# Gate sums and first maxima inside the convolution units, and r, k, v as three products of rounded parts

## The reference

```
# layer 0: gated short convolution beside forgetting attention (8 heads x 64)
z = x @ w_in;  ax, a_b, a_c, q, k, v, fl = split(z)
y_a  = a_b * conv3(a_c * ax)                        # causal, width 3
logf = log_sigmoid(fl + b_f);  cum = cumsum(logf)
s = q.k / 8 + cum[query] - cum[key], masked;  o = softmax(s) @ v
y = concat(y_a, o) @ w_out
# layer 1: RWKV-7 time mixing (16 heads x 64)
xr, xw, xk, xv, xa, xg = (x + (x_prev - x) * mu[n] for n in range(6))
r = xr @ w_r;  k = xk @ w_k;  v = xv @ w_v          # 1024 x 1024 each
# w, a, g: products through a narrow hidden layer; then a recurrence over the positions
# every layer ends in a SwiGLU channel mixer and a gated embedding
```

## Time and profile before

| what | value |
|---|---|
| median of 3 runs | 4127.3 us (4125.62 to 4127.95) |
| profiled execution | 4123.89 us |
| its span | 4122.3 us |
| TensorE busy | 3726.8 us, 90% |
| VectorE busy | 1461.3 us, 35% |
| ScalarE busy | 831.4 us, 20% |
| POOL busy | 203.2 us, 5% |

### The profile page before, as it was taken

One profiled execution on the slowest core, in us unless ns is written; L12 is line 12 of the kernel. 1 busy time (PEld: TensorE's weight loads), 2 busy tenths in 40 slices (PEclk: granted clock), 3 DMA queues, 4 the chain that ended last, 5 costly groups with the idle time before them and its releaser, 6 DMA issues.

```text
span 4122.3 us, 64833 instructions
## 1 busy us (share of the span) xinstructions
PE 3726.8 (90%) x27922; PEld 3201.6 (78%) x27922; DVE 1461.3 (35%) x1951; ACT 831.4 (20%) x1107; POOL 203.2 (5%) x345
## 2 busy tenths in 40 slices
PE   7998899899999998878998868889797999999977
PEld 4996337789999998754564537878496999999967
DVE  3123544342212223432211645555635222222352
ACT  2000232210000001223311423333322000000021
POOL 0001000000000000000000211111100000000000
PEclk9998999999999999986999989999999999999989
DMA  2212002111121131002222652211311112112211
GB/s 87 73 53 85 21 21 76 70 45 41 46 83 48 46 124 47 29 21 107 96 74 103 258 187 54 53 45 52 139 42 69 46 36 73 62 46 87 77 37 69
DMA packets 75064, 291.43 MB, mean 71 GB/s; under 512 B 9368, under 2 KB 11688, under 8 KB 71128
## 3 DMA queue, kind: packets, MB, share of 16 engines
q0 software_dynamic: 36528, 165.56, 11.1%
q1 hardware_dynamic: 38336, 122.87, 9.6%
HBM read 211.77 MB, written 76.62 MB: 70 GB/s over the span
## 4 chain that ended last, share of the span: by engine, by line
PE 72%; DVE 8%; ACT 2%; issue 2%; DMA 1%; POOL 0%; DVEq 0%; ACTq 0%; POOLq 0%
PE ps L443 47%; PE ps L417 11%; DVE A L1436 2%; PE ps L836 2%; PE ps L845 2%; DVE B L1436 1%; PE ps L750 1%; PE ps L457 1%; DVE H L1517 1%; PE ps L796 1%; DVE A_r L1493 1%; PE ps L475 1%; DVE B L1900 1%; PE ps L859 1%; PE ps L823 1%
## 5 line engine op out<-in xcount | busy, mean ns | idle before, releaser
L443 PE MATMUL ps<-A_r,TM_r 128*128 128x364 f32 x2736 | 605.3, 329 | 0.0
L443 PE MATMUL ps<-H_r,W_r 128*128 128x364 f32 (+1 forms) x2616 | 576.3, 328 | 0.0
L443 PE MATMUL ps<-H_r,TM_r 128*128 128x364 f32 x2352 | 520.8, 329 | 19.0 <-DVE A_r L1493 19.0
L417 PE MATMUL ps<-B,W 128*128 128x364 f32 (+1 forms) x1488 | 469.7, 477 | 24.9 <-DVE B L1436 24.9
L443 PEld LDWEIGHTS ps<-A_r,TM_r 128*128 128x128 f32 x2736 | 476.0, 189 | 0.0
L443 PEld LDWEIGHTS ps<-H_r,W_r 128*128 128x128 f32 (+1 forms) x2616 | 453.5, 187 | 1.8
L417 PEld LDWEIGHTS ps<-B,W 128*128 128x128 f32 (+1 forms) x1488 | 282.5, 190 | 207.6 <-issue 28.7
L443 PEld LDWEIGHTS ps<-H_r,TM_r 128*128 128x128 f32 x2352 | 408.0, 188 | 23.7 <-issue 14.5
L443 PE MATMUL ps<-B_r,DW_r 128*128 128x364 f32 x2112 | 408.8, 329 | 0.0
L443 PE MATMUL ps<-B_r,W_r 128*128 128x364 f32 x1824 | 404.6, 330 | 0.0
L443 PEld LDWEIGHTS ps<-B_r,DW_r 128*128 128x128 f32 x2112 | 358.8, 188 | 0.0
(11 more groups left out here) (279 smaller groups left out, 4146.4 us busy)
## 6 DMA issues: line engine op xcount, KB each, us to landing
W<-in_wgu SPq DMA_DIRECT2D x88, 512.0 KB, 3.6
W<-in_wdown SPq DMA_DIRECT2D x32, 384.0 KB, 3.1
W<-in_wrkv SPq DMA_DIRECT2D x24, 512.0 KB, 3.7
W<-in_wdown SPq DMA_DIRECT2D x32, 320.0 KB, 2.9
d_h<-H POOLq DMA_DIRECT2D x16, 546.0 KB, 3.0
d_y<-TM POOLq DMA_DIRECT2D x16, 546.0 KB, 3.6
A<-d_y POOLq DMA_DIRECT2D x16, 546.0 KB, 7.8
H<-d_h POOLq DMA_DIRECT2D x2, 4368.0 KB, 22.7
```

What stands on the lines that cost most here:

```text
L417: ins = nc.tensor.matmul(ps[0:cols, NCH * s + c, 0:CH], W[0:rows, slot, j * cols:(j + 1) * cols], xs[n][0:rows, c * CH:(c + 1) * CH], star ...
L443: ins = nc.tensor.matmul(ps[0:cols, NCH * s + c, 0:CH], w[:, j * cols:(j + 1) * cols], x[k1][:, c * CH:(c + 1) * CH], start=(k1 == 0 and n ...
```

## The change

**Layer 0.** The gate's log f and running sums move ahead of the convolution loop on ScalarE and VectorE, and `turn_sums` stands between the third and the fourth convolution unit. The filler products go. Behind each of the last nine convolution units TensorE computes one piece of the first pair's scores, in banks 6 and 7, and VectorE reduces it among the steps of the convolution; pieces 9 to 11 stay behind the last unit, and both `spread` calls follow them. POOL sends the sums and loads the bias rows of the first pair between the convolution's stores; the other pairs' rows stay behind the last unit. The gate's buffers move from A and TM to B and DW.

**Layer 1.** r, k and v use `split_unit`. The upper parts of the mixed activations are written to H, the remainders in place in B. H is therefore stored to memory when layer 0 ends and loaded again when the recurrence has begun. VectorE splits every weight tile; in the v loop the split stands behind the first instruction of a pair. Results of r and k leave through two buffers where there were four, and so do those of v.

The diff, cut to its core:

```diff
-                 "down": (DWr[:, 0, :], DWr[:, 1, :])}
+                 "down": (DWr[:, 0, :], DWr[:, 1, :]),
+                 "rkv": (TMr[:, 2, 0:KT * P], TMr[:, 3, 0:KT * P]),
+                 "value": (Br[:, 20, 0:KT * P], Br[:, 21, 0:KT * P])}
...
-        BIAS = [Af[:, SEQ * h:SEQ * h + SEQ] for h in range(HF)]
-        TOP = [[Af[:, HF * SEQ + 16 * b + 8 * h:HF * SEQ + 16 * b + 8 * h + 8] for h in range(2)] for b in range(2)]
+        BIAS = [Bf[:, 12 * T + SEQ * h:12 * T + SEQ * h + SEQ] if h < 2 else Af[:, SEQ * h:SEQ * h + SEQ] for h in range(HF)]
+        full, cump = Bf[0:HF, 12 * T:12 * T + NALL], Bf[0:HF, 12 * T + NALL:12 * T + NALL + SEQ]
+        DWf = DW[:, :, :].rearrange("p a n -> p (a n)")
...
-        CKT = Tf[:, 3200:3200 + 8 * (8 + NBLK)].rearrange("p (k h) -> p k h", h=HF)
-        zcol = Tf[:, 3500:3501]
+        CKT = Bf[:, o_ + 32:o_ + 32 + 8 * (8 + NBLK)].rearrange("p (k h) -> p k h", h=HF)
+        zcol = Bf[:, o_ + 240:o_ + 241]
...
             split_unit(xh, xl, cols=HF)
-            for j in range(3 * NA):
-                split_unit(xh, xl)
...
                 qb, n0, n = ROWS[j]
+                bank = 0 if p else 6
                 if pieces(p, j):
                     pe.wait_ge(S["s_read"], pieces(p, j))
-                if halves(p, int(j >= FIRST_HALF[0])):
+                else:
+                    pe.wait_ge(S["ckt_ready"], 1)
+                if p:
                     pe.wait_ge(S["mb_read"], halves(p, int(j >= FIRST_HALF[0])))
...
+            for j in range(3 * NA):
+                split_unit(xh, xl)
+                if j == 2:
+                    turn_sums()
+                if j >= 3:
+                    scores(0, j - 3)
+
             pe.wait_ge(S["read0"], t.val("read0"))
             pe.wait_ge(S["read1"], t.val("read1"))
-            full_clock(16)
-            turn_sums()
-            for j in range(len(ROWS)):
+            for j in range(3 * NA - 3, len(ROWS)):
                 scores(0, j)
-                if j == FIRST_HALF[0] - 1:
-                    spread(0, 0)
+            spread(0, 0)
             spread(0, 1)
             turned(0, 0)
             turned(0, 1)
...
+            xh = [Hr[:, j, :] for j in range(KT)]
+            xlow = [[Br[:, 8 * b + j, :] for j in range(KT)] for b in range(2)]
+            enter(t, "rkv")
             for n in range(2):
-                pe.wait_ge(S["xn_ready"], t.up("xn_ready", KT))
-                xs = X[(n + 1) % 2]
-                dense8(KT)
...
+                t.up("xn_ready", KT)
+                split_units(KT, xh, xlow[(n + 1) % 2])
...
+            enter(t, "value")
+            pe.wait_ge(S["xl_ready"], t.up("xl_ready", KT))
...
-                    unit([KT], xs)
+                    split_unit(xh, xlow[1])
...
+            z, e = B[0:HF, 15, :], DWf[0:HF, 0:T]
+            s, mm, rd = t.unit()
...
             for c in range(NA):
+                if c == 1:
+                    turned_sums()
...
-            turned_sums()
...
+            def upper_mixed(b, kt):
+
+                act.wait_ge(S["xn_ready"], t.val("xn_tmp", kt + 1 - KT))
+                nc.scalar.activation(Hr[:, kt, :], B[:, 8 * b + kt, :], ACT.Copy).then_inc(S["xh_ready"], 1)
...
             mix(0)
-            stage()
+            act.wait_ge(S["hs_out"], 16)
+            for n in range(KT):
+                staged(n, 4)
+                upper_mixed(1, n)
             mix(2)
-            stage()
-            mix(3)
-            stage()
+            for n in range(KT):
+                staged(n, 2)
+            for n in range(KT):
+                upper_mixed(0, n)
+            for n in range(KT):
+                if n < 2:
+                    mix(3, 4 * n, 4 * n + 4)
+                staged(n, 2)
+            for n in range(KT):
+                upper_mixed(1, n)
...
+            lf, e = B[0:HF, 15, :], DWf[0:HF, 0:T]
+            step(nc.vector.memset(zcol, 0.0))
+            dve.wait_ge(S["lf_e"], 1)
+            step(stt(lf, lf, 0.0, e, ALU.min, ALU.subtract))
+            dve.wait_ge(S["cum_in"], t.up("cum_in", 16))
+            step(nc.vector.tensor_copy(full[:, PAST:NALL], lf[:, S0:T]))
+            nc.vector.tensor_tensor_scan(cump, lf[:, P0:P0 + SEQ], zcol[0:HF].to_broadcast([HF, SEQ]), 0.0, ALU.add,
+                                         ALU.subtract)
+            step(nc.vector.tensor_tensor_scan(full, full, zcol[0:HF].to_broadcast([HF, NALL]), 0.0, ALU.add, ALU.subtract))
+            step(nc.vector.tensor_scalar(cump, cump, -8.0, None, ALU.mult))
+            nc.vector.tensor_scalar(full, full, -8.0, None, ALU.mult).then_inc(S["cum_ready"], 1)
...
             for c in range(NA):
                 s, mm, rd = t.unit()
                 dve.wait_ge(S[f"read{s}"], rd)
                 split_chunk()
+                if c:
+                    reduced(0, 3 * c - 3)
...
                 step(nc.vector.memset(TM[:, 2, 0:PAD], 0.0))
+                if c:
+                    reduced(0, 3 * c - 2)
...
                 if c < NA - 1:
                     split_chunk()
...
+                if c:
+                    reduced(0, 3 * c - 1)
...
             dve.wait_ge(S["ckt_ready"], 1)
-            for j in range(len(ROWS)):
+            for j in range(3 * NA - 3, len(ROWS)):
                 reduced(0, j)
-            nc.vector.memset(zcol, 0.0)
+            dve.wait_ge(S["s_read"], len(ROWS))
+            dve.wait_ge(S["logf_out"], 1)
+            dve.wait_ge(S["conv_out"], 32 * NA)
+            nc.vector.memset(B[:, 12:16, 0:PAD], 0.0)
+            nc.vector.memset(B[:, 12:16, S0 - PAD:S0], 0.0)
...
+            def lower_mixed(b):
+
+                for kt in range(KT):
+                    dve.wait_ge(S["xh_ready"], t.up("xh_ready"))
+                    nc.vector.tensor_tensor(Br[:, 8 * b + kt, :], B[:, 8 * b + kt, :], Hr[:, kt, :],
+                                            ALU.subtract).then_inc(S["xl_ready"], 1)
+                    t.up("xl_ready")
...
+            def split_weights(done):
+
+                slot, landed = t.chunk()
+                if done:
+                    dve.wait_ge(S["mm_done"], done)
+                dve.wait_ge(S[f"w{slot}"], landed)
+                w, wh = W[:, slot, 0:KT * P], wh_of(t)
+                step(nc.vector.tensor_copy(wh, w))
+                nc.vector.tensor_tensor(Wr[:, slot, 0:KT * P], w, wh, ALU.subtract).then_inc(S["wl_ready"], 1)
...
+            enter(t, "rkv")
+            mix(0, 1)
+            mix(1, 4)
+            mix(2, 5)
+            mix(3, 0)
+            split_weights(0)
+            lower_mixed(1)
+            split_weights(0)
+            mix(4, 2)
+            for m in range(2, KT + 1):
+                split_weights(mm0 + 27 + m - 1)
+            lower_mixed(0)
+            split_weights(mm0 + 27 + KT)
+            dve.wait_ge(S["mm_done"], read_by[3])
+            step(nc.vector.memset(B[:, 8:16, 0:1], 0.0))
+            mix(5, 3, 0, 4)
+            split_weights(mm0 + 27 + KT + 1)
+            mix(5, 3, 4, 8)
+            for m in range(KT + 3, 2 * KT):
+                split_weights(mm0 + 27 + m - 1)
+            enter(t, "value")
+            dve.wait_ge(S["xs2"], 96)
+            dve.wait_ge(S["xs3"], 96)
+            lower_mixed(1)
...
                     step(nc.vector.tensor_scalar(tmpA, L["a"], vec[:, V["ka"], bass.ds(pair, 1)],
                                                  kab[:, bass.ds(pair, 1)], ALU.mult, ALU.add))
+                    split_weights(0)
                     dve.wait_ge(S["key_scaled"], t.up("key_scaled"))
...
+            dve.wait_ge(S["hs_in"], 16)
             channel_mixer(1)
...
+            pool.dma_start(full[:, 0:PAST], I["clogf"]).then_inc(S["cum_in"], 16)
...
+            pool.wait_ge(S["cum_ready"], 1)
+            pool.dma_start(d_cum, cump).then_inc(S["cum_out"], 16)
+            pool.dma_start(d_cums, full).then_inc(S["cum_out"], 16)
+            store(O["logf"], B[0:HF, 15, :])
+            pool.wait_ge(S["cum_out"], 32)
+            pool.wait_ge(S["ckt_done"], 1)
+            bias(0)
+            pool.wait_ge(S["out_done"], t.val("out_done"))
+            pool.sem_inc(S["logf_out"], 1)
             for c in range(NA):
...
             pool.wait_ge(S["mm_done"], t.val("mm_done"))
-            pool.dma_start(Af[0:HF, 5000:5000 + PAST], I["clogf"]).then_inc(S["cum_in"], 16)
...
+            for i in range(1, NA):
+                pool.wait_ge(S["bias_in0"], 32 * i)
+                bias(i)
...
+            pool.wait_ge(S["h_ready"], 24)
+            pool.dma_start(d_h, H[:, :, :]).then_inc(S["hs_out"], 16)
             pool.wait_ge(S["shift_in"], 1)
...
             for name in "rk":
-                keep(name)
+                with t.loop(4, mm_done=2, read0=1, read1=1, xs0=16, xs1=16) as i:
...
             double_chunk(2)
+            pool.wait_ge(S["hs_out"], 16)
+            pool.dma_start(H[:, :, :], d_h).then_inc(S["hs_in"], 16)
             with t.loop(3, u_done=8, tok_done=8, zi0=96, zi1=96) as i:
```

(53 more changed lines are left out.)

119 lines of the change are left out of this document (42 added, 77 removed).

## The result

The changed kernel takes 4086.44 us (median of 3 runs, 4082.80 to 4092.95) where the kernel before takes 4127.3: a ratio of 0.990 (0.9885 to 0.9912). The prediction was 4026, with a range of 4010 to 4052. The sign was right; 60 us of the gain are missing. The profiled execution took 4082.8.

A forecast was written before the change was run, and what follows sets the result against it. TensorE, 72% of the span, bounds it: stages pay only where it computes or stands on the chain. 41.3 + 38.1 + 21.8 = 101.2 off 4123.9 gives 4022.7; with the median 3.4 higher, 4026, range 4010 to 4052.

The forecast's parts named there:

- H's reload: Recurrence: loading H again takes 22.7 us, fits between two of POOL's chunk loads and costs nothing.
- A: v loop: transfers set its period, so it gives nothing; 4048, chance 0.14.
- B: First stage: half the gain, with turning at its old price and nine pieces waiting for VectorE; 4045, chance 0.10.
- C: All changed stages: weight splits come a unit late, 3.5 us at each of 33 units; slower, 4142, chance 0.06.
- D: Attention of layer 0: key or bias rows wait for POOL, so the first stage's 41.3 go; 4067, chance 0.04.
- r and k: Layer 1: sixteen units shrink from 14.68 to 11.95 us; net gain 38.1 after a later start and the gap.
- v loop: Layer 1: eight pairs each 2.73 us shorter, with idle and low clock between units unchanged; gain 21.8.
- about 1: v loop: cover in us left to a pair's loads before ScalarE's key step, from about 4 before.
- Turning: First stage: TensorE turns the gate sums between dense convolution units at full clock, 5.1 us (ends 5.1 and 10.2).
- Pieces: First stage: score pieces 0 to 7 with causal additions add 7.6 us of TensorE between convolution units.
- Tail: First stage: 18 us from the last convolution unit to the first transposed score (ends 15.4 and 23.5).
- The stage as a whole: Layer 0, last convolution unit to first transposed score: 72.0 us before, gain 41.3 (ends 30.7 and 43.9).

The follow-up runs named there:

- badly placed even kernel: The changed kernel with TensorE's recurrence written out as 17 chunks of 1,280 instructions and 16 added waits before it: 4072.98 us, ratio 0.987.
- well placed one: The changed kernel with TensorE's recurrence written out as 17 chunks of 1,280 instructions and 154 added waits before it: 4025.70 us, ratio 0.975.
- last two kernels: The changed kernel with TensorE's recurrence written out as 17 chunks of 1,280 instructions, with 154 or 16 added waits before it: 4025.70 and 4072.98 us.
- first placement between: The changed kernel with H reloaded behind the recurrence and 66 added waits in TensorE's program before it: 4063.44 us (2 runs).

## Why the prediction was wrong

**The step that failed** is one that the prediction did not take: it gave the recurrence a single term, H's reload, "so it fits between and I cost it at nothing". The reload was indeed worth nothing that the medians show. But TensorE's longer program moved the boundaries of the instruction packets, and the recurrence took 53.4 more in the profile; moving them back by 134 instructions returned 53 us of the time. No rival held it: A to D all lie ahead of the recurrence. Rows that hinted at it were there, TensorE's "issue" stalls inside rows of like products in the recurrence before (10 of them, 14.5 us), and went unread.

**With the placement undone** the forecast's mechanism and most of its size stand: 4033.45 against 4026, inside the range. The 7 that are missing are about what the turning and the v loop fell short by in the profile of the change (5.4 and 3.0). Term by term, in that profile:

- r and k: 38.1 predicted, 38.0 in the profile (72.67 by the end of k, less 34.63). The gap (3.7) came out at 3.59, the slow first tiles (1.4) at 1.8, the units at 11.97. The 0.5 by which r was to start later did not come.
- v loop: 21.8 predicted, 18.8 measured. The units shrank by 3.0 each (TensorE's busy time less its sums, 15.2 to 12.1), a little more than said, but the eight first sums take 29.5 together where they took 24.2: the granted clock is 0.90 in the loop, 0.93 before. "Low clock included" assumed that it stays as it was. Of the loads' "about 1" nothing was left once: the fifth pair's key step starts at 2253.30, right behind its load (2240.04 to 2253.16), and TensorE idles 3.66 there where it idles 3.48.
- Turning: 5.1 predicted "between dense units ... at the full one". It took 8.0, and 2.5 more in the units behind it, in all 10.5, just past the upper end of 10.2. During its 50 products with 8 columns the clock fell (0.70 there, 0.55 behind it).
- Pieces: 7.6 predicted; the last unit ends 18.5 later, counted from the start of the convolution units, and less the 10.5 that is 8.0.
- Tail: 18 predicted, 14.3 in this profile, 16.7 to 18.0 in the other ten profiles with this part of the change. The clock stayed at 1.00 in this one.
- The stage as a whole: 41.3 predicted (from 72.0, which its own rows give as 71.9), 39.4 at the first transposed score, 34.4 at the output projection. The 5.0 between are not rival D: the attention takes 269.7 here and 264.7 before, but 270.5 in the kernel with the edits of layer 1 alone, and 262.7 in that with layer 0 alone. It varies with the granted clock from profile to profile: 0.96, 0.98, 0.96 and 0.99 in these four.
- Splits of weights, bias rows, the conv stores, costed at nothing: no wait of TensorE for them shows in the first stage, in the units of r and k or in the v loop.

Rivals A (v loop gives nothing), B (half of the first stage) and C (late splits) are refuted by 18.8, by the 35.1 of that half alone and by units of 11.97; the 35.1 also speaks against D.

**What stays open.** Which idle time tips the clock: in the badly placed even kernel a wait of 1.63 for VectorE is followed, one row on, by sixteen products in 1.02, in the well placed one by sixteen in 0.68, and only the short stalls earlier in the chunk differ. And what else, beside the chunk's loads, makes packets late; and whether the reload costs its 10 us at the bad placement.

## What to carry to other kernels

Lengthening one engine's program moves the packet boundaries of the stages behind it; where a stage issues many short instructions, as here (16 products in 0.47 us), read its "issue" stalls inside rows of like instructions before trusting its time to stay. When a stage with unchanged code gets slower, pad the engine's program by part of a packet under an existing wait and by a whole one as control: here the whole one cost nothing that shows (4081.09 against 4086.44), and the two together told placement from all that stays the same. The loop, 5,152 instructions in the trace and no multiple of 256, brought the same places again in each of its three rounds; written out, the chunks kept their places at 1,280 each, and one good choice served all of them.

## What the runs showed of the hardware

- 134 instructions placed under a wait changed the time by 53 us, 256 by nothing that shows; in the kernel before, 122 cost 45 us.
- A stall for instructions ended 1.2 to 1.6 us after its 16 KB packet had landed (changed kernel), and the fetch ran less than one packet of 256 ahead (at most 212 instructions, last two kernels). The jump back of the loop cost 3.1 to 4.7 us of idle where it showed, and none of that is left when the loop is written out. The Trainium skill (Runtime: NRT & Kernel Launch, section "Instruction fetch mechanics") says that a taken branch out of the held blocks forces such a fetch, and these stalls agree.
- The total of the stalls does not give their price: 49.6 us of them (first placement between) went with a recurrence of 481.8, 24.1 us (even, bad place) with 497.7. In the first, TensorE's waits for VectorE at line 807 fall to 4.1 us, from 26.6 in the second: so most of its stalls stand where TensorE would have waited anyway. It is busy 409.9 and 423.4, at granted clocks of 0.93 and 0.92.
